# Three output panels worked abreast, k-tile by k-tile, at four stage changes of a two-block transformer kernel

## Chip, cores and metric

The kernel runs on one core of a Trainium2 chip. The metric is device time in microseconds (us) of one execution; lower is better. Below, PE is TensorE, DVE is VectorE, ACT is ScalarE, POOL is GpSimd and SP is SyncE.

## The reference

Two blocks follow each other on 256 tokens of width 1024, all in fp32. The first is an RMS norm, an input projection, several mixers (gated linear attention, cross attention) and an output projection. The second puts 16 meta tokens ahead (272 rows) and runs

```python
h = h + 0.5 * rmsnorm(swiglu(rmsnorm(h, n[0]), ffn1_wi[l], ffn1_wo[l]), n[1])
h = h + rmsnorm(hybrid_mixer(rmsnorm(h, n[2]), w_in[l], ...), n[3])
h = h + 0.5 * rmsnorm(swiglu(rmsnorm(h, n[4]), ffn2_wi[l], ffn2_wo[l]), n[5])
```

where swiglu multiplies by a 1024 x 5632 matrix and then by a 2816 x 1024 one, and hybrid_mixer begins with the projection of its normed input. What matters here is that each of these projections begins with a norm of the whole hidden state.

## The kernel before

Activations lie transposed, features on partitions: 8 k-tiles of 128 features by 256 or 272 columns (rows of the sequence). Weights come as panels of 1024 columns (one output tile of 128 features by 8 k-tiles). A panel passes a ring of 4 slots (RING): SP loads it into `raw`, ACT copies it to `whi` in a reduced-precision form (L648), POOL subtracts to get the rest, `wlo` (L553), and PE multiplies. The activation is split the same way, into `xh` (ACT) and `xl` (DVE). So each k-tile of an output costs three matmuls, and an output of 8 k-tiles costs 24, summed in one of four PSUM banks (`pb[o % 4]`).

`output` does one such output: it waits for the panel's `wlo` and for the bank (`open_output`), and then does the k-tiles in order. At a stage change its `each` argument makes each k-tile wait for its `xl`. DVE reads the finished bank, and only then is the bank free again.

The norm's scale is applied behind the matmuls, when a bank is read. Its statistic is the sum of squares: ACT squares each k-tile (`pre_norm`), POOL adds the squares (`sum_squares`), PE sums over partitions (`norm_stat`, L1470), ACT takes the root (`pre_root`, L669 and L671) into `xrstd`. DVE reads no bank of the new stage before that.

Every engine works through its own list in the order in which it is written. This order sets when panels are ready. On ACT the panels of a new stage are copied up to LEAD = 3 ahead, so its first three are split when the stage begins; the copy of the fourth stands behind `pre_root` in ACT's list:

```python
            pre_norm(3, combined(0), "gains", 0, WOUT_O + 7)
            pre_root(3)
            ...
            ahead(UP1_P - 1)
            up_loop(0, UP1_O, LEN)
```

`ahead(UP1_P - 1)` reaches panel UP1_P + 2, and the first `high_in_loop` of `up_loop` copies panel UP1_P + 3. A copy also waits until the panel that held its slot has been multiplied (`passed`).

The four places of the change are the starts of: UP1 (44 outputs of 272 columns, norm 3), the mixer (12 qkv outputs of 272 columns, norm 5), OUT2 (the mixer's output projection, 8 outputs of 256 columns, without a norm ahead, its `xl` made from `mg`), and UP2 (44 outputs of 256 columns, norm 7). In the mixer, the step `("logits",)` multiplies `h` by the small `wba` (L1695) into `ba`, transposes that (L1701), and DVE and ACT make `grate` from it (`g_ready`); the step `("cumulate",)` waits for that. On DVE each qkv output is scaled into `pre` (L1272) and then convolved in three instructions (`conv_tile`: L1227, L1231, L1236). Behind OUT2 and the down projections DVE runs `take_in`: for each output a copy out of PSUM (L1009), its square (L1011) and a sum (L1016).

Of the kernel before, what the change touches and what calls it, by code (L numbers as in the profile page):

```python
# [5 lines left out]
ROWS = 256  # L6
META = 16
LEN = META + ROWS
KT = 8
# [6 lines left out]
RING = 4  # L16
LEAD = 3
# [8 lines left out]
OUT2_P = MIX_P + 56 + 12  # L26
# [6 lines left out]
OUT2_O = MIX_O + 56 + 24  # L33
# [136 lines left out]
MIX_OUT = mixer_outputs()  # L170
# [49 lines left out]
def build(nc, a):  # L220
# [3 lines left out]
    with ctx:  # L224
# [22 lines left out]
        xh = at("xh", take(KT * LEN), [P, KT, LEN], f32r)  # L247
        xl = at("xl", take(KT * LEN), [P, KT, LEN], f32r)
# [51 lines left out]
        qkv = at("qkv", ar, [P, 12, LEN])  # L300
# [51 lines left out]
        pb = [ctx.enter_context(nc.psum_tensor(f"panel{i}", [P, 512], f32)) for i in range(4)]  # L352
# [12 lines left out]
        passed = sem("passed")  # L365
# [80 lines left out]
        mg_low = sem("mg_low")  # L446
# [1013 lines left out]
        def _(pe):  # L1460
            M = nc.tensor.matmul

            def norm_stat(n):

                bank, use = aux("stat", n)
                y = squares_of(n)
                late = n in (2, 4, 6, 8)
                aux_open(use)
                pe.wait_ge(summed, n + 1)
                ins = M(bank[:, 0:W[n]], ones[:], y[:, 0, 0:W[n]], start=True, stop=not late)  # L1470
                if late:
                    pe.wait_ge(last_squared, n // 2)
                    ins = M(bank[:, 0:W[n]], ones[:], y[:, KT - 1, 0:W[n]], start=False, stop=True)
                if n == 0:
                    for rt in range(2):
                        ins = M(bank[:, ROWS + rt:ROWS + rt + 1], y[:, 0, P * rt:P * rt + P], ones[:, 0:1], start=True, stop=True)
                ins.then_inc(aux_full, 1)

            def products(bank, slot, pairs, hi_, lo_, c0, w, first, last, each=None):
                for m, (t, kk) in enumerate(pairs):  # L1480
                    if each is not None:
                        each(kk)
                    for n, (wt, x) in enumerate(((whi, hi_), (whi, lo_), (wlo, hi_))):
                        ins = M(bank[:, 0:w], wt[:, slot, P * t:P * t + P], x[:, kk, c0:c0 + w],  # L1484
                                start=first and m == 0 and n == 0, stop=last and m == len(pairs) - 1 and n == 2)
                return ins

            def tiles_split(n):

                return lambda kk: pe.wait_ge(split_low, 8 * SPLIT[n] + kk + 1)  # L1490

            def open_output(o, p):

                pe.wait_ge(lo_ready, p + 1)
                if o >= 4:
                    pe.wait_ge(bank_free[o % 4], o // 4)

            def output(o, p, hi_, lo_, w, c0=0, tiles=KT, half=0, each=None):

                open_output(o, p)  # L1500
                pairs = [(tiles * half + t, t) for t in range(tiles)]
                products(pb[o % 4], p % RING, pairs, hi_, lo_, c0, w, True, True, each).then_inc(passed, 1)

            def output_rows(o, p, hi_, lo_):


                if p % 2:
                    return
                open_output(o, p)
                open_output(o + 1, p + 1)  # L1510
                r = p % RING
                for rt in range(2):
                    for kk in range(KT):
                        for n, (wt, x) in enumerate(((whi, hi_), (whi, lo_), (wlo, hi_))):
                            ins = M(pb[(o + rt) % 4][:, 0:2 * P], x[:, kk, P * rt:P * rt + P],  # L1515
                                    wt[:, r:r + 2, P * kk:P * kk + P], start=kk == 0 and n == 0, stop=kk == KT - 1 and n == 2)
                ins.then_inc(passed, 2)
# [29 lines left out]
            for step in FIRST:  # L1547
                kind, i = step[0], step[-1]
                if kind == "lowrank":
                    bank, n = aux("lowrank")  # L1550
                    aux_open(n)
                    for kk in range(KT):
                        ins = M(bank[0:16, 0:ROWS], wglr[:, kk, :], tmp[:, kk, 0:ROWS], start=kk == 0, stop=kk == KT - 1)
# [3 lines left out]
                if kind == "decay":  # L1557
                    aux_freed(pe, AUX[("lowrank",)])
                    for x in range(2):
                        bank, n = aux("up", x)  # L1560
                        aux_open(n)
                        for t in range(2):
                            ins = M(bank[:, 256 * t:256 * t + 256], upw[:, P * (2 * x + t):P * (2 * x + t) + P], glr[:],
                                    start=True, stop=True)
                        ins.then_inc(aux_full, 1)
                if kind == "level":
# [7 lines left out]
                    for x in range(2):  # L1574
                        if l == 8 and x:
                            break
                        bank, n = aux("level", l, g, x)
                        aux_open(n)
                        for m in range(4):
                            if l < 8:  # L1580
                                hd, blk = 4 * g + 2 * x + m // 2, slice(P * (m % 2), P * (m % 2) + P)
                                ins = M(bank[:, P * m:P * m + P], k[:, hd, blk], q[:, hd, blk], start=True, stop=True)  # L1582
                            else:
                                ins = M(bank[:, P * m:P * m + P], k[:, 4 * g + m, 0:P], q[:, 4 * g + m, P:ROWS], start=True, stop=True)
# [5 lines left out]
                if kind == "scores":  # L1590
                    st, pair = i // 2, i % 2
                    bank, n = aux("scores", i)
# [4 lines left out]
                    for e in range(2):  # L1597
                        ins = M(bank[:, ROWS * e:ROWS * e + ROWS], xq[:, 2 * pair + e, P * st:P * st + P], mk[:, 2 * pair + e, :],
                                start=True, stop=True)
                    ins.then_inc(aux_full, 1)  # L1600
                if kind == "probs":
                    bank, n = aux("probs", i)
# [4 lines left out]
                if kind == "o":  # L1607
                    bank, n = aux("o", i)
# [14 lines left out]
                    for e in range(2):  # L1623
                        if i < 6:
# [4 lines left out]
                            ins = M(bank[:, ROWS * e + P:ROWS * e + ROWS], v[:, 1, col:col + P], s[:, hd, P:ROWS],  # L1629
                                    start=False, stop=True)  # L1630
# [6 lines left out]
                if kind == "o_norm":  # L1637
                    bank, n = aux("o_norm", i)
# [13 lines left out]

            def up_loop(first_o, first_p, w, norm):

                output(first_o, first_p, xh, xl, w, each=tiles_split(norm))
                norm_stat(norm)
                for n in range(1, 4):
                    output(first_o + n, first_p + n, xh, xl, w)
                with pe.Fori(0, UP // 4 - 1) as g:
                    for n in range(4):  # L1660
                        pe.wait_ge(lo_ready, g * 4 + (first_p + 4 + n + 1))
                        pe.wait_ge(bank_free[n], g + (first_o // 4 + 1))
                        products(pb[n], n, [(t, t) for t in range(KT)], xh, xl, 0, w, True, True).then_inc(passed, 1)
# [21 lines left out]
            for step in MIXER:  # L1685
# [17 lines left out]
                if kind == "cumulate":  # L1703
# [3 lines left out]
                    for d in range(2):  # L1707
                        M(bank[0:CH, 16 * d:16 * d + 16], tri[:, d, :], grate[:, :, 4 * d:4 * d + 4], start=True, stop=True)
                    M(bank[0:CH, 32:64], ones[0:CH, 0:CH], small2[0:CH, 96:128], start=True, stop=True).then_inc(aux_full, 1)
                if kind in ("qkv", "fourier_in", "sconv"):  # L1710
                    output(o, p, xh, xl, LEN, each=tiles_split(5) if step == ("qkv", 0) else None)
                    if step == ("qkv", 0):
                        norm_stat(5)
                if kind in ("z", "gate"):
                    output(o, p, xh, xl, ROWS, META)
                if kind == "branch":
# [132 lines left out]
                if kind == "delta_norm":  # L1849
                    for e in range(2):  # L1850
# [3 lines left out]
                        for m in range(2):  # L1854
                            ins = M(bank[:, ROWS * m:ROWS * m + ROWS], ones[:], dsq[:, 2 * e + m, :], start=True, stop=True)
                        ins.then_inc(aux_full, 1)
            for i in range(8):
                output(OUT2_O + i, OUT2_P + i, xh, xl, ROWS, each=(lambda kk: pe.wait_ge(mg_low, kk + 1)) if i == 0 else None)
            norm_stat(6)
            up_loop(UP2_O, UP2_P, ROWS, 7)  # L1860
            down_loop(1, DOWN2_O, DOWN2_P, ROWS)
# [119 lines left out]
```

## Time and profile before

| | before |
|---|---|
| median of 3 executions | 1151.41 us (1149.96 to 1151.47) |
| span of the profiled execution | 1152.5 us |
| PE busy | 1028.8 us, 89% of the span |
| POOL busy | 746.5 us, 65% |
| DVE busy | 640.1 us, 56% |
| ACT busy | 472.7 us, 41% |

The profile is of one execution. Its span, from the first instruction to the last, is all the time that is known of it; it stands 1.1 us above the median. A matmul's row lasts longer than its share of PE, since matmuls overlap: the pace is the distance between the starts of neighbours. Two matmul rows stand for one fp32 product (L1470, L1695).

### The profile page before, as it was taken

Reading aid. Unit: us, or ns where it says so; the run is one execution under the profiler, and the core shown is the slowest. Engines: PE = TensorE matmul, PEld = TensorE weight load, DVE = VectorE, ACT = ScalarE, POOL = GpSimd, SP = SyncE. Lnnn points to the kernel's source line nnn. Section 1 sums busy time; section 2 is a strip of 40 time slices with the busy share of each in tenths; the row PEclk is TensorE's granted clock in tenths of the full one; section 3 lists DMA queues with packets and bytes.
Section 4 is the critical chain, followed back from the end, with each engine's and each line's share of the span. In section 5 each row is a group of like instructions: output and inputs, shape, how many; then the busy total and the mean of one; then the engine's idle time right before and its main releaser. Section 6 shows DMA issues by size and latency. Waiting matters only on the chain.

```text
span 1152.5 us, 21258 instructions
## 1 busy us (share of the span) xinstructions
PE 1028.8 (89%) x8096; PEld 998.8 (87%) x8096; DVE 640.1 (56%) x1026; ACT 472.7 (41%) x698; POOL 746.5 (65%) x349
## 2 busy tenths in 40 slices
PE   5799999989899999997988294999999869999996
PEld 4699999989799999996988174999999859999995
DVE  6324994447755554447955053345555585666454
ACT  5344224444454444444464012433325445444441
POOL 3786555647778878984767022655635757888993
PEclk9899999999899999997988696999998978999998
DMA  7454333425445555652441122443323633665561
GB/s 254 135 176 134 117 119 119 132 90 164 147 144 167 167 179 165 189 181 86 147 134 51 5 60 48 146 133 107 97 87 94 199 110 116 197 183 183 173 196 66
DMA packets 52368, 155.44 MB, mean 135 GB/s; under 512 B 10228, under 2 KB 15612, under 8 KB 52108
## 3 DMA queue, kind: packets, MB, share of 16 engines
q1 hardware_dynamic: 45504, 151.28, 42.3%
q10 hardware_dynamic: 6800, 3.25, 1.2%
q8 instruction: 47, 0.77, 0.3%
q14 instruction: 17, 0.14, 0.0%
HBM read 152.11 MB, written 2.39 MB: 134 GB/s over the span
## 4 chain that ended last, share of the span: by engine, by line
PE 75%; DVE 15%; ACT 3%; ACTq 3%; DMA 1%; issue 1%; POOL 1%; DVEq 0%; SPq 0%
PE panel L1484 58%; PE panel L1515 4%; PE aux L1582 2%; ACTq L871 2%; DVE xl L968 1%; PE aux L1771 1%; DVE qkv L1231 1%; DVE qkv L1236 1%; ACTq L885 1%; DVE qkv L1227 1%; DVE pr L1313 1%; DMA tm<-inverses 1%; DVE h L983 1%; POOL wlo L553 1%; DVE tmp L978 1%
## 5 line engine op out<-in xcount | busy, mean ns | idle before, releaser
L553 POOL TENSOR_TENSOR wlo<-raw,whi 128x1024 fp32r<-128x1024 f32 x284 | 700.5, 2486 | 343.1 <-ACT whi L648 343.1
L1484 PE MATMUL panel<-xh,whi 128*128 128x256 f32 (+1 forms) x1504 | 443.6, 295 | 27.0 <-DVE xl L968 18.8
L1484 PE MATMUL panel<-xl,whi 128*128 128x256 f32 (+1 forms) x1504 | 435.3, 289 | 0.0
L1484 PE MATMUL panel<-xh,wlo 128*128 128x256 f32 (+1 forms) x1504 | 434.3, 289 | 0.0
L648 ACT ACTIVATE whi<-raw 128x1024 fp32r<-128x1024 f32 x284 | 294.0, 1052 | 204.8 <-PE panel L1484 148.8
L1484 PEld LDWEIGHTS panel<-xh,whi 128*128 128x128 f32 x1504 | 291.7, 194 | 35.8 <-DVE xl L968 14.2
L1484 PEld LDWEIGHTS panel<-xh,wlo 128*128 128x128 f32 x1504 | 291.7, 194 | 0.0
L1484 PEld LDWEIGHTS panel<-xl,whi 128*128 128x128 f32 x1504 | 291.2, 194 | 0.5
L1484 PE MATMUL panel<-hh,whi 128*128 128x272 f32 (+1 forms) x352 | 100.1, 284 | 0.0
L1484 PE MATMUL panel<-hh,wlo 128*128 128x272 f32 (+1 forms) x352 | 99.9, 284 | 0.0
L1484 PE MATMUL panel<-hl,whi 128*128 128x272 f32 (+1 forms) x352 | 99.8, 284 | 0.0
L1206 DVE TENSOR_TENSOR hl<-hid,hh 128x272 f32 (+1 forms) x44 | 53.4, 1213 | 32.9 <-ACT hh L795 32.9
L1204 DVE TENSOR_TENSOR hid<-hid,sil 128x272 f32<-128x272 f32 (+1 forms) x44 | 66.1, 1502 | 6.6 <-ACT sil L793 1.0
L795 ACT ACTIVATE hh<-hid 128x272 f32 (+1 forms) x44 | 18.7, 425 | 123.2 <-DVE hid L1204 123.2
L1484 PEld LDWEIGHTS panel<-hl,whi 128*128 128x128 f32 x352 | 66.4, 189 | 0.0
L1484 PEld LDWEIGHTS panel<-hh,wlo 128*128 128x128 f32 x352 | 66.2, 188 | 0.0
L1484 PEld LDWEIGHTS panel<-hh,whi 128*128 128x128 f32 x352 | 66.1, 188 | 0.0
L1200 DVE TENSOR_TENSOR hid<-panel,xrstd 128x272 f32<-128x272 f32 (+1 forms) x44 | 19.1, 433 | 65.1 <-PE panel L1484 65.1
L1009 DVE COPY tmp<-panel 128x256 f32<-128x256 f32 (+1 forms) x24 | 10.3, 430 | 76.0 <-PE panel L1484 75.9
L1016 DVE TENSOR_TENSOR sq<-sq 128x256 f32<-128x256 f32 (+1 forms) x24 | 44.4, 1850 | 0.8
L1484 PE MATMUL panel<-mixh,whi 128*128 128x256 f32 x128 | 37.3, 292 | 4.1 <-DVE mixl L1178 4.1
L1771 PE MATMUL aux<-cmat,pf 68*128 68x256 f32 x64 | 18.2, 448 | 22.2 <-DVE pf L1339 22.2
(286 smaller groups left out, 1603.2 us busy)
## 6 DMA issues: line engine op xcount, KB each, us to landing
raw<-in_panels SPq DMA_DIRECT2D x236, 512.0 KB, 3.5
raw<-in_down SPq DMA_DIRECT2D x32, 448.0 KB, 3.3
raw<-in_down SPq DMA_DIRECT2D x16, 512.0 KB, 3.6
memx<-in_mem SPq DMA_DIRECT2D x1, 1024.0 KB, 5.1
h<-in_x SPq DMA_DIRECT2D x1, 1024.0 KB, 8.2
spill<-h ACTq DMA_DIRECT2D x1, 1024.0 KB, 6.2
h<-spill ACTq DMA_DIRECT2D x1, 1024.0 KB, 7.3
out<-h SPq DMA_DIRECT2D x2, 512.0 KB, 2.9
```

Of the source, the lines that this page charges most:

```text
L553: nc.gpsimd.tensor_tensor(wlo[:, slot, :], raw[:, slot, :], whi[:, slot, :].bitcast(f32), ALU.subtract).then_inc(lo_ready, 1)
L648: A(whi[:, slot, :], raw[:, slot, :], ACT.Copy).then_inc(hi_ready, 1)
L795: A(hh[:, bass.ds(tile, 1), 0:w].rearrange("p a s -> p (a s)"), hid[:, pair, 0:w], ACT.Copy).then_inc(hid_high, 1)
L871: act.dma_start(a["blocks"][b].rearrange("m i j -> i m j"), am[at_b, :, :, at_b].rearrange("i u h j -> i (u h) j")).then_inc(blocks_in, 16)
L1016: ins = TT(sq[:, 0, 0:W[n]], sq[:, 0, 0:W[n]], sq[:, i, 0:W[n]], ALU.add)
L1200: TT(hid[:, pair, 0:w], pb[2 * pair + 1][:, 0:w], xrstd[:, 0:w], ALU.mult)\
L1204: TT(hid[:, pair, 0:w], hid[:, pair, 0:w], sil[:, pair, 0:w], ALU.mult).then_inc(hid_ready, 1)
L1206: TT(hl[:, bass.ds(tile, 1), 0:w].rearrange("p a s -> p (a s)"), hid[:, pair, 0:w], hh[:, bass.ds(tile, 1), 0:w].rearrange("p a s -> p (a ...
L1484: ins = M(bank[:, 0:w], wt[:, slot, P * t:P * t + P], x[:, kk, c0:c0 + w], start=first and m == 0 and n == 0, stop=last and m == len(pairs ...
L1515: ins = M(pb[(o + rt) % 4][:, 0:2 * P], x[:, kk, P * rt:P * rt + P], wt[:, r:r + 2, P * kk:P * kk + P], start=kk == 0 and n == 0, stop=kk ...
L1582: ins = M(bank[:, P * m:P * m + P], k[:, hd, blk], q[:, hd, blk], start=True, stop=True)
L1771: ins = M(bank[:, 0:ROWS], pf[:, i % 2, c, P * cs:P * cs + P], cmat[:, c, cs, :], start=x == 0 and m == 0, stop=x == 1 and m == 3)
```

## The change

A new function `outputs_abreast` opens three outputs (three banks, three panels), and then does, for each k-tile, three matmuls for each of them. It takes the place of `output` for the first three outputs at the four places. `norm_stat` now stands behind all three. In the mixer, qkv 1 and qkv 2 are done with qkv 0, ahead of the logits, and the steps `("qkv", 1)` and `("qkv", 2)` leave PE nothing to do.

```diff
+            def outputs_abreast(outputs, hi_, lo_, w, each):
+
+                for o, p in outputs:
+                    open_output(o, p)
+                for kk in range(KT):
+                    each(kk)
+                    for o, p in outputs:
+                        ins = products(pb[o % 4], p % RING, [(kk, kk)], hi_, lo_, 0, w, kk == 0, kk == KT - 1)
+                        if kk == KT - 1:
+                            ins.then_inc(passed, 1)
...
             def up_loop(first_o, first_p, w, norm):
 
-                output(first_o, first_p, xh, xl, w, each=tiles_split(norm))
+                outputs_abreast([(first_o + n, first_p + n) for n in range(LEAD)], xh, xl, w, tiles_split(norm))
                 norm_stat(norm)
-                for n in range(1, 4):
+                for n in range(LEAD, 4):
                     output(first_o + n, first_p + n, xh, xl, w)
...
-                if kind in ("qkv", "fourier_in", "sconv"):
-                    output(o, p, xh, xl, LEN, each=tiles_split(5) if step == ("qkv", 0) else None)
-                    if step == ("qkv", 0):
-                        norm_stat(5)
+                if step == ("qkv", 0):
+                    outputs_abreast([MIX_OUT[("qkv", n)][:2] for n in range(LEAD)], xh, xl, LEN, tiles_split(5))
+                    norm_stat(5)
+                elif kind in ("qkv", "fourier_in", "sconv") and step not in (("qkv", 1), ("qkv", 2)):
+                    output(o, p, xh, xl, LEN)
...
-            for i in range(8):
-                output(OUT2_O + i, OUT2_P + i, xh, xl, ROWS, each=(lambda kk: pe.wait_ge(mg_low, kk + 1)) if i == 0 else None)
+            outputs_abreast([(OUT2_O + i, OUT2_P + i) for i in range(LEAD)], xh, xl, ROWS, lambda kk: pe.wait_ge(mg_low, kk + 1))
+            for i in range(LEAD, 8):
+                output(OUT2_O + i, OUT2_P + i, xh, xl, ROWS)
```

The order of instructions changes on PE alone; DVE, ACT and SP have the same lists before and after, and POOL's differs in nothing but line numbers. On PE at UP1, before, the last k-tile of the first output, the statistic (L1470), and then the second output (panel1 is its bank):

```order
L1484 MATMUL panel0<-xh_52,whi_50 128x272 [waits split_low]
L1484 MATMUL panel0<-xl_53,whi_50 128x272
L1484 MATMUL panel0<-xh_52,wlo_51 128x272
L1470 MATMUL aux0<-sq_56,ones_61 128x272 [waits summed,aux_free0]
L1484 MATMUL panel1<-xh_52,whi_50 128x272 [waits bank_free1,lo_ready]
L1484 MATMUL panel1<-xl_53,whi_50 128x272
L1484 MATMUL panel1<-xh_52,wlo_51 128x272
```

Of the change, the last k-tile of all three, the statistic, and then the fourth output:

```order
L1484 MATMUL panel0<-xh_52,whi_50 128x272 [waits split_low]
L1484 MATMUL panel0<-xl_53,whi_50 128x272
L1484 MATMUL panel0<-xh_52,wlo_51 128x272
L1484 MATMUL panel1<-xh_52,whi_50 128x272
L1484 MATMUL panel1<-xl_53,whi_50 128x272
L1484 MATMUL panel1<-xh_52,wlo_51 128x272
L1484 MATMUL panel2<-xh_52,whi_50 128x272
L1484 MATMUL panel2<-xl_53,whi_50 128x272
L1484 MATMUL panel2<-xh_52,wlo_51 128x272
L1470 MATMUL aux0<-sq_56,ones_61 128x272 [waits summed,aux_free0]
L1484 MATMUL panel3<-xh_52,whi_50 128x272 [waits bank_free3,lo_ready]
```

The statistic has moved behind six more matmuls of the last k-tile (and behind 48 more in all), and what follows it is the output of the fourth panel, which waits for that panel's `wlo`.

On PE at the mixer's start, before, the end of qkv 1, the logits (L1695, then the transposes of `ba`, L1701), and qkv 2 (panel2):

```order
L1484 MATMUL panel1<-xh_52,whi_50 128x272
L1484 MATMUL panel1<-xl_53,whi_50 128x272
L1484 MATMUL panel1<-xh_52,wlo_51 128x272
L1695 MATMUL aux3<-h_54,wba_64 16x272 [waits wba_scaled,aux_free3]
L1695 MATMUL aux3<-h_54,wba_64 16x272 x7
L1701 MATMUL aux0<-ident_60,ba_119 68x16 [waits aux_free0,aux_free3]
L1701 MATMUL aux0<-ident_60,ba_119 68x16 x3
L1484 MATMUL panel2<-xh_52,whi_50 128x272 [waits bank_free2,lo_ready]
```

Of the change, the end of the three, the statistic, the logits (now L1706 and L1712), the cumulate step (L1719, which waits for `g_ready`), and qkv 3 (panel3):

```order
L1484 MATMUL panel2<-xh_52,whi_50 128x272
L1484 MATMUL panel2<-xl_53,whi_50 128x272
L1484 MATMUL panel2<-xh_52,wlo_51 128x272
L1470 MATMUL aux2<-sq_56,ones_61 128x272 [waits summed,aux_free2]
L1706 MATMUL aux3<-h_54,wba_64 16x272 [waits wba_scaled,aux_free3]
L1706 MATMUL aux3<-h_54,wba_64 16x272 x7
L1712 MATMUL aux0<-ident_60,ba_119 68x16 [waits aux_free0,aux_free3]
L1712 MATMUL aux0<-ident_60,ba_119 68x16 x3
L1719 MATMUL aux1<-small2_117,tri_65 68x16 [waits g_ready,aux_free1]
L1719 MATMUL aux1<-small2_117,tri_65 68x16
L1720 MATMUL aux1<-small2_117,ones_61 68x32
L1484 MATMUL panel3<-xh_52,whi_50 128x272 [waits bank_free3,lo_ready]
```

Nothing stands any longer between the statistic and the logits, nor between the logits and the cumulate step, where qkv 1 and qkv 2 stood.

## Rows read from the trace of the kernel before

**Rows 1.** Page, the chain that ended last, shares by engine.

```profile
PE 75%; DVE 15%; ACT 3%; ACTq 3%; DMA 1%; issue 1%; POOL 1%; DVEq 0%; SPq 0%
```

**Rows 2.** Waits, whole trace, then 903 to 960: who waited for whom, us, times, longest.

```profile
PE panel L1484 <- DVE xl L968: 18.8, 20, 3.8
...
PE panel L1484 <- DVE xl L1450: 4.2, 2, 2.5
```

**Rows 3.** Chain in order of time: start us, us, what; changes to UP1 and UP2.

```profile
316.57 1.73 PE panel L1484 x6
...
319.20 196.28 PE panel L1484 x1560
...
952.52 1.65 PE panel L1484 x6
...
955.02 185.65 PE panel L1484 x1560
```

**Rows 4.** Timeline at UP1: start us, us, engine, line, op, [idle before <-releaser].

```profile
308.74 0.36 PE L1484 MATMUL panel<-xh,whi 128*128 128x272 f32 x1 [2.80 <-DVE xl L968]
...
315.51 1.41 DVE L968 SCALAR_TENSOR_TENSOR xl<-h,vec,xh 128x272 fp32r<-128x272 f32 x2
...
319.24 0.49 ACT L669 ACTIVATE lnt<-aux,vec 128x272 f32<-128x272 f32 x1 [2.77 <-PE aux L1470]
...
321.50 2.01 ACT L648 ACTIVATE whi<-raw 128x1024 fp32r<-128x1024 f32 x2
...
322.65 20.13 POOL L553 TENSOR_TENSOR wlo<-raw,whi 128x1024 fp32r<-128x1024 f32 x8 [5.10 <-ACT whi L648]
```

**Rows 5.** Windows: us, PE busy, PEclk, DMA share, GB/s; the granted clock.

```profile
319.00:320.00 1.00, 1.00 (x8) 0.81 0.00 0
...
520.00:521.00 1.00, 0.00 (x0) 0.88 0.00 0
...
916.00:917.00 1.00, 1.00 (x7) 0.65 0.00 0
...
957.00:958.00 1.00, 1.00 (x8) 0.67 0.00 0
```

**Rows 6.** Timeline at UP1, PE: two neighbouring matmuls at the lower clock.

```profile
317.41 0.43 PE L1484 MATMUL panel<-xh,whi 128*128 128x272 f32 x1
...
317.64 0.43 PE L1484 MATMUL panel<-xl,whi 128*128 128x272 f32 x1
```

**Rows 7.** Timeline at the mixer's start.

```profile
536.88 3.84 PE L1695 MATMUL aux<-h,wba 128*16 128x272 f32 x16
...
534.53 0.44 DVE L1272 TENSOR_TENSOR pre<-panel,xrstd 128x272 f32<-128x272 f32 x1 [3.37 <-ACT xrstd L671]
...
537.47 0.93 DVE L1227 TENSOR_SCALAR qkv<-pre,vec 128x272 f32<-128x272 f32 x1
...
538.32 2.58 DVE L1231 SCALAR_TENSOR_TENSOR qkv<-pre,vec,qkv 128x271 f32<-128x271 f32 x1
...
540.82 0.42 DVE L1247 TENSOR_TENSOR ba<-aux,xrstd 16x272 f32<-16x272 f32 x1
...
535.87 4.73 POOL L553 TENSOR_TENSOR wlo<-raw,whi 128x1024 fp32r<-128x1024 f32 x2 [4.07 <-ACT whi L648]
```

**Rows 8.** Timeline: POOL, four splits back to back, and one VectorE operation among them.

```profile
550.07 10.02 POOL L553 TENSOR_TENSOR wlo<-raw,whi 128x1024 fp32r<-128x1024 f32 x4 [0.68 <-ACT whi L648]
...
552.78 2.64 DVE L1236 SCALAR_TENSOR_TENSOR qkv<-pre,vec,qkv 128x271 f32<-128x271 f32 x1
```

**Rows 9.** Timeline at OUT2.

```profile
908.33 0.36 PE L1484 MATMUL panel<-xh,whi 128*128 128x256 f32 x1 [2.47 <-DVE xl L1450]
...
912.42 0.39 PE L1484 MATMUL panel<-xh,whi 128*128 128x256 f32 x1 [1.73 <-DVE xl L1450]
...
913.50 1.06 ACT L648 ACTIVATE whi<-raw 128x1024 fp32r<-128x1024 f32 x1 [4.01 <-PE panel L1484]
...
914.63 2.37 POOL L553 TENSOR_TENSOR wlo<-raw,whi 128x1024 fp32r<-128x1024 f32 x1 [2.55 <-ACT whi L648]
...
933.20 2.37 POOL L553 TENSOR_TENSOR wlo<-raw,whi 128x1024 fp32r<-128x1024 f32 x1 [0.27 <-ACT whi L648]
...
937.61 0.42 DVE L1011 TENSOR_TENSOR sq<-tmp 128x256 f32<-128x256 f32 x1
```

**Rows 10.** Timeline at UP2, POOL.

```profile
958.43 14.94 POOL L553 TENSOR_TENSOR wlo<-raw,whi 128x1024 fp32r<-128x1024 f32 x6 [4.98 <-ACT whi L648]
```

## The prediction

> **What bounds the kernel now.** I read the page's chain first. PE holds 75% of it [rows 1], so time is won where PE waits with work at hand. The list of waits says how much of that lies at the stage changes: PE waited 18.8 us in all for an `xl` of a norm, and 4.2 us for an `xl` of OUT2 [rows 2]. That is what the change can fill. The chain in order of time then shows what follows such a wait: from 319.20 on, 1560 matmuls in 196.28 us without a break, 0.126 us each, and at UP2 1560 from 955.02 in 185.65 us, 0.119 each [rows 3]. So in UP1 and UP2 every microsecond by which PE starts its unbroken run earlier is won, and every one later is lost. Then the timelines of the other engines at the four places, to see what that run waits for.
>
> **The term that decides: the fourth panel.** The change brings forward two outputs, 48 matmuls or 6.0 us at UP1. But PE can go on only if the fourth panel is split by then. In ACT's list its copy stands behind the root of the statistic: Ln at 319.24, table load, copies from 321.50, and POOL takes the first at 322.65, after 5.10 us without work [rows 4]. At 20.13/8 = 2.5 us a split, it is ready at 325.15. Before, PE had outputs 2 and 3 to do in that time: 319.20 + 48 x 0.126 = 325.25 [rows 3]. The cover fits to a tenth. Now both are done ahead of the statistic, and the cover is gone: PE stands still from the statistic to the fourth panel, 5.9 us (325.15 - 319.24). What is saved ahead of the statistic is given back behind it, but for the shift of the statistic itself.
>
> **The clock.** Where PE has idled, its granted clock falls: at 520 to 521 PE is idle and the mean clock 0.88, so it fell in that microsecond from 2.4 GHz to 1.2 (0.5) [rows 5]. It rises again under work. At UP1 unbroken work began at 316.57 [rows 3] and the clock rose at 319.4 (0.81 in that microsecond is 38% at 0.5), 2.8 us later; at OUT2, where a pause of 1.73 us brought the lower clock, at 912.42 [rows 9] and 916.7, 4.3 us; at UP2 at 952.52 and 957.7, 5.1 us [rows 3, 5]. I take 4.0 us, bounds 2.8 and 5.1. A matmul of 272 columns takes 0.225 us at the lower clock (317.41 to 317.64, rounded) [rows 6] against 0.126, so 4.0 us there cost 4.0 x (1 - 0.126/0.225) = 1.8 us (1.2 to 2.2). After 5.9 us of idleness the fourth output starts at the lower clock, and nothing hides that: it heads the unbroken run.
>
> **UP1: +2.6.** The first matmul is at 308.74 [rows 4]. 72 matmuls: 4.0 us at 0.225 do 17.8, the other 54.2 take 6.8 us, more than the k-tiles need to arrive (the last `xl` ends at 316.92) [rows 4]. They end at 319.55. The statistic's two matmuls take 0.5 (3.84/16 each at the full clock) [rows 7], so it ends at 320.05 against 319.20: 0.85 late. ACT, and POOL behind it, shift by as much, and the fourth output starts at 326.1 where it started at 325.25. With the clock: 0.85 + 1.8 = +2.6 us. Bounds with 2.8 and 5.1: +1.5 and +3.6.
>
> **UP2: +1.0.** Here k-tiles come slower, and the last two set the end: 18 matmuls from 952.52 take 2.1 us at the full clock, the statistic 0.5: 955.15 against 955.02. The fourth panel is ready at 958.43 + 2.5 + 0.15 = 961.1 [rows 10]. Before, the fourth output started at 955.02 + 2.64 at 0.213 (12.4 matmuls; 0.225 x 256/272) + 35.6 x 0.119 = 961.9. So PE begins 0.8 earlier, and pays 1.8 for the clock: +1.0 (+0.4 to +1.6).
>
> **OUT2: +1.4.** No norm stands here, and PE does gain: the three outputs run without a break from 908.33, the wait of 1.73 at 912.42 [rows 9] is filled, and no idleness lowers the clock. They end at 908.33 + 72 x 0.119 = 916.9. But the first output now ends at 908.33 + 66 x 0.119 + 0.3 = 916.5, not 913.4, and the copy of the fifth panel waits for exactly that (ACT, 913.50, released by PE). POOL's row of splits, which began at 914.63, begins at 917.6; the copies of two more panels are released at once, and from then POOL runs seven splits back to back. They set what DVE can do: a VectorE operation with its inputs in SBUF that meets a split waits for its end. In the mixer four splits took 10.02 us, 2.5 each, and the operation among them 2.64 instead of 0.42 to 0.49 [rows 8]; 538.32 shows the same [rows 7]. Seven splits end at 935.1 (before 935.57). `take_in` has 14 such operations. The first fits in ahead of the splits, seven pass, one a split, and six are left behind them, with three copies: nine at 0.455 us are 4.1 us, so it ends at 939.4 (935.1 + 0.3 + 4.1, rounded down), against 938.03 [rows 9]. PE's last output would be done by 916.9 + 5 x 2.85 = 931.2. If operations slip between splits, it is less. If VectorE were not held at all, `take_in` would follow PE; before, the three outputs ended at about 912.42 + 54 x 0.119 + 1.8 (the clock) = 920.6, so PE is some 3.5 us earlier. I take +1.4, ends -3.5 and +2.0, near the held end because the rows are of two-input operations like these.
>
> The Trainium skill (SBUF — State Buffer, Who interferes with whom) has the rule for it: a VectorE instruction with two SBUF inputs contends with a GpSimd one that reads SBUF. The trace agrees (2.64 us). The same section says that the order of issue decides who is blocked; if VectorE came first each time, OUT2 would be worth its -3.5 and the whole sum 0.1 us. In rows 7 and 8 it was VectorE that was held.
>
> **The mixer's start: 0.** DVE sets the pace here. The statistic is 0.3 late by the reckoning of UP2. qkv 1 is then at hand, so its operations move up from 537.47 to about 536.1, just where POOL's first split starts (535.87 + 0.3). If the scaling (L1227) slips in first, the next operation is held by one split and not by the second, and `ba` comes at 538.8 and not 540.82, -2.0. If it doesn't, `ba` comes at 541.3, +0.5 [rows 7]. The logits' matmuls (3.84 us) used to follow qkv 1, and now follow the statistic and end at 537.8, in time. But PE has then only small work until `g_ready`, and qkv 3 runs at the lower clock: 24 matmuls take 4.8 us, not 3.0, and DVE may wait up to 1 us for it. Range -2.0 to +1.5; between two cases of unlike sign I take 0.
>
> **Parts at no cost.** Opening three outputs at once needs three panels split: OUT2's third is the closest, and PE begins only after DVE's first `xl`, when it is. Their banks have long been read. PE changes banks between k-tiles elsewhere at the same pace. SP and the DMAs follow `wlo`; a load has at least one split of 2.5 us to spare.
>
> **Sum.** 2.6 + 0 + 1.4 + 1.0 = +5.0 us. The profiled span of 1152.5 us becomes 1157.5. It stands 1.1 above the median, so the median of 1151.4 becomes 1156.4. A measurement tells about 0.2%, 2.3 us, from no change.
>
> **Rivals.**
> 1. *VectorE keeps up at OUT2, and the mixer falls well.* -3.5 to 0 at OUT2 and -2 to 0 in the mixer, beside +3.6 of UP1 and UP2: from -1.9 up to the edge of what can be told, +2.3, so 1149.5 to 1153.7. In its middle, 1151.6, it is no change. For: some operations before a split began passed at 0.42. Chance 0.20.
> 2. *The change pays (other side).* It needs one thing: that the clock survives the 5.9 us of idleness at UP1 and UP2, or that the matmuls abreast reach the full clock sooner than the sparse ones did. Then UP1 is +0.85 or less, UP2 -0.8, and with PE's gain at OUT2, -3.5, the sum is -3.5, 1148; it decides from a clock that costs under 1 us a place. Against: rows 5 show it fall while PE idled, and the pause of 1.73 us at OUT2 was enough. Chance 0.10.
> 3. *The clock stays low through the whole of the matmuls abreast*, because PE still pauses for k-tiles. 72 x 0.225 = 16.2 us: UP1's statistic ends near 308.74 + 16.2 + 1 = 326, 6.8 late; the mixer's and UP2's, with slower k-tiles, some 5 late each. With OUT2 and the clock behind the idleness the sum is about +20, 1171. Against: with nine matmuls a k-tile at 0.225, 2.0 us, and a k-tile every 1.3 to 1.7, PE has no pauses while it is slow, and unbroken work raised the clock in all three rows. Chance 0.05. The Trainium skill speaks for this rival (TensorE: Matmul & The Clock Gate, "A second HAM failure mode: psum-queue depth-cycling"): a kernel that cycled through PSUM banks paused PE often enough between groups that its clock went up and down. No run here shows it for groups that stand back to back.
> 4. *The change doesn't do what it says*, PE still waits as before: excluded by the order, which has nine matmuls between waits.
>
> **Chances.** Forecast 0.65 (1153.7 to 1160), rivals 0.20, 0.10, 0.05. Faster by over 0.2%: rival 2 and the low end of rival 1, 0.10. Within: 0.22. Slower: 0.68. The range for 8 in 10 runs from 1152 (leaves rival 2 and half of rival 1) to 1160 (the bounds of the terms, 3.6 + 1.6 + 2.0 + 1.5 = 8.7).
>
> **What the new profile would show.** PE idle 5 to 6 us behind L1470 at UP1 and UP2, released by POOL `wlo`, and the clock at 0.5 behind it; the waits for `xl` at a third or less. At OUT2, POOL without a gap and L1011 and L1016 at 2.5 us each. Wrong would be: no idle PE behind the statistic (the fourth panel came another way), or a clock of 1.0 there.

## The result, and the profile after

The changed kernel takes 1157.68 us in the median (1157.21 to 1158.83, 4 runs), beside 1151.44 us for the kernel before on the same chip (1149.96 to 1153.64, 4 runs). The ratio is 1.0055, 95% interval 1.0038 to 1.0071: slower by 6.2 us by the medians. I had put 1156.4, range 1152 to 1160.

The page, the chain by engine, and the list of waits (who waited for whom, us in total, times, longest), changed kernel:

```profile
PE 75%; DVE 12%; ACT 4%; ACTq 3%; issue 2%; POOL 2%; DMA 1%; DVEq 0%; SPq 0%; POOLq 0%
...
PE panel L1484 <- POOL wlo L553: 27.1, 6, 13.1
...
PE panel L1484 <- DVE xl L968: 11.4, 7, 3.8
```

DVE's share of the chain fell from 15% to 12% [rows 1] and PE's wait for `xl` from 18.8 us to 11.4 [rows 2]: the change did what it was made for. What came in its place is in the same two rows. POOL's share went from 1% to 2%, "issue" from 1% to 2%, and PE waits 27.1 us for `wlo` where it waited 18.3 before; some 14 us of either sum belong to the start of the program, and the two new waits are of 5.8 us each.

The waits for `xl` did not fall to "a third or less". At each of the four places PE waits once for the first k-tile, 2.5 to 3.8 us, and bringing other outputs forward cannot fill that; of the 20 waits of norms before, 7 are left, and these carry 11.4 of the 18.8 us.

The chain in order of time (start us, us, what), changed kernel, at UP1 and UP2:

```profile
316.42 6.65 issue
...
323.11 2.35 POOL wlo L553
...
325.51 192.03 PE panel L1484 x1512
...
953.76 6.02 issue
...
959.81 2.35 POOL wlo L553
...
962.21 181.35 PE panel L1484 x1512
```

Before, the unbroken run was 1560 matmuls from 319.20 [rows 3]. Now it is 1512, two outputs fewer, and begins at 325.51, behind POOL's split. The timeline of ACT and POOL there (start us, us, engine, line, op, [idle before <-releaser]):

```profile
319.71 0.49 ACT L669 ACTIVATE lnt<-aux,vec 128x272 f32<-128x272 f32 x1 [3.54 <-PE aux L1470]
...
321.97 2.00 ACT L648 ACTIVATE whi<-raw 128x1024 fp32r<-128x1024 f32 x2
...
323.11 7.42 POOL L553 TENSOR_TENSOR wlo<-raw,whi 128x1024 fp32r<-128x1024 f32 x3 [5.84 <-ACT whi L648]
```

The whole row of ACT and POOL has moved by about half a microsecond against [rows 4] (Ln from 319.24 to 319.71), and PE stands still from the statistic to the end of the first split: 325.46 - 319.71 = 5.8 us, where I had written 5.9. The clock in that stretch (window us, PE busy, PEclk, DMA share, GB/s):

```profile
320.00:321.00 1.00, 0.00 (x0) 1.00 0.00 0
...
322.00:323.00 1.00, 0.00 (x0) 0.73 0.00 0
...
329.00:330.00 1.00, 1.00 (x9) 0.85 0.69 94
```

It falls to 1.2 GHz while PE idles, and is back at 2.4 in the microsecond 329 to 330, some 4 us into the new run.

OUT2 of the changed kernel, timeline:

```profile
916.07 2.96 ACT L648 ACTIVATE whi<-raw 128x1024 fp32r<-128x1024 f32 x3 [7.00 <-PE panel L1484]
...
917.20 17.59 POOL L553 TENSOR_TENSOR wlo<-raw,whi 128x1024 fp32r<-128x1024 f32 x7 [4.84 <-ACT whi L648]
...
917.26 2.63 DVE L1011 TENSOR_TENSOR sq<-tmp 128x256 f32<-128x256 f32 x1
...
919.93 2.51 DVE L1016 TENSOR_TENSOR sq<-sq 128x256 f32<-128x256 f32 x1
...
922.47 0.43 DVE L1009 COPY tmp<-panel 128x256 f32<-128x256 f32 x1
...
938.66 0.43 DVE L1011 TENSOR_TENSOR sq<-tmp 128x256 f32<-128x256 f32 x1
```

POOL's first split went from 914.63 [rows 9] to 917.20, seven stand back to back, and every square and sum that meets one takes 2.0 to 2.6 us. The copy between them, which reads PSUM, takes 0.43. The mixer's start, changed kernel:

```profile
538.31 4.97 POOL L553 TENSOR_TENSOR wlo<-raw,whi 128x1024 fp32r<-128x1024 f32 x2 [4.40 <-ACT whi L648]
...
538.49 2.59 DVE L1231 SCALAR_TENSOR_TENSOR qkv<-pre,vec,qkv 128x271 f32<-128x271 f32 x1
...
541.00 0.42 DVE L1247 TENSOR_TENSOR ba<-aux,xrstd 16x272 f32<-16x272 f32 x1
...
551.29 0.44 DVE L1272 TENSOR_TENSOR pre<-panel,xrstd 128x272 f32<-128x272 f32 x1 [1.86 <-PE panel L1484]
```

Only one operation is held, by the first of the two splits. Before, it was held by the second, and the scaling ahead of it by half a microsecond by the first [rows 7].

Where the time went shows best in the length of stages. Each number is the distance between two rows: the starts of ACT's exponentials (L671) that bound a stage, of ACT's first square of qkv in the mixer (L841), and of PE's first matmul of OUT2. "Before again" is the kernel before, profiled once more beside the experiments.

| stage, us | before | before again | after |
|---|---|---|---|
| norm 2 to UP1's root | 13.27 | 13.26 | 14.06 |
| UP1's root to norm 4 | 198.26 | 198.94 | 199.84 |
| norm 4 to the mixer's root | 15.98 | 15.98 | 16.38 |
| mixer's root to its first L841 | 29.55 | 29.87 | 26.82 |
| OUT2: first matmul to norm 6 | 31.64 | 28.74 | 33.11 |
| norm 6 to UP2's root | 15.60 | 15.59 | 15.93 |
| UP2's root to norm 8 | 187.31 | 187.06 | 188.81 |

### The profile page after: what moved, and what is told of

Read it like the earlier page. It is cut to its first block, busy times and chain, and to the rows that moved or that the text cites. A ratio compares the mean times of both kernels' runs of the same rounds, so it can differ in the third digit from the quotient of the medians.

```text
span 1155.4 us, 21258 instructions
## 1 busy us (share of the span) xinstructions
PE 1021.2 (88%) x8096; PEld 995.0 (86%) x8096; DVE 640.0 (55%) x1026; ACT 472.4 (41%) x698; POOL 746.4 (65%) x349
## 4 chain that ended last, share of the span: by engine, by line
PE 75%; DVE 12%; ACT 4%; ACTq 3%; issue 2%; POOL 2%; DMA 1%; DVEq 0%; SPq 0%; POOLq 0%
PE panel L1484 59%; PE panel L1526 4%; PE aux L1593 2%; ACTq L871 2%; POOL wlo L553 1%; PE aux L1783 1%; DVE xl L968 1%; ACTq L885 1%; DVE sq L1011 1%; DVE pr L1313 1%; DMA tm<-inverses 1%; DVE tmp L978 1%; DVE h L983 1%; DVE sq L1016 1%; PE aux L1840 1%
## 5 line engine op out<-in xcount | busy, mean ns | idle before, releaser
L1206 DVE TENSOR_TENSOR hl<-hid,hh 128x272 f32 (+1 forms) x44 | 50.5, 1148 | 32.9 <-ACT hh L795 32.9
L1016 DVE TENSOR_TENSOR sq<-sq 128x256 f32<-128x256 f32 (+1 forms) x24 | 48.5, 2021 | 0.8
```

Of the source, the lines that this page charges most:

```text
L1016: ins = TT(sq[:, 0, 0:W[n]], sq[:, 0, 0:W[n]], sq[:, i, 0:W[n]], ALU.add)
L1206: TT(hl[:, bass.ds(tile, 1), 0:w].rearrange("p a s -> p (a s)"), hid[:, pair, 0:w], hh[:, bass.ds(tile, 1), 0:w].rearrange("p a s -> p (a ...
```

## Experiments

Each was timed against the kernel before on the same chip. The stage lengths are those of the one profiled execution of each kernel.

### The kernel before, once more

> The kernel before, unchanged, measured against itself on the same chip: 0 us within 0.2%. It shows how far two profiles of one kernel differ stage by stage, which the comparison of the single profiles of before and after needs; I expect the mixer to differ by up to 3 us and the other stages by under 0.5.

1151.47 us (12 runs), ratio 1.0003, 0.999 to 1.0016. But its single executions lie between 1148.9 and 1156.0, and the profiled one has a span of 1148.5, 4.0 less than the profile that I had argued from. Two stages are shorter by more than that: 2.7 us in the mixer between the l2 norm and `zs` (62.97 and 65.68), where nothing was changed, and 2.9 at OUT2; the others add 1.6 the other way. OUT2 in this execution:

```profile
906.90 2.76 DVE L1450 TENSOR_TENSOR xl<-mg,xh 128x256 fp32r<-128x256 f32 x8
...
933.83 0.43 DVE L1011 TENSOR_TENSOR sq<-tmp 128x256 f32<-128x256 f32 x1
```

The eight `xl` take 2.76 us in one go. In my profile a split fell among them, they took 4.93, PE paused for 1.73 us and its clock fell to the lower level (0.50 at 914 to 915) [rows 9]. Of the profiles with OUT2 in the old order and nothing changed there, this one and that of the mixer's start alone have 28.7 us; mine has 31.64, and two more, each the slowest execution of its kernel, 30.1 and 30.6. I had taken a slow draw for the stage's length. The split among the `xl` is not the whole of it: in the 30.1 the eight `xl` took 2.76 us too, and what made that stage longer stays open.

### UP1 and UP2 alone

Only `up_loop` has the three abreast:

```diff
-                output(first_o, first_p, xh, xl, w, each=tiles_split(norm))
+                outputs_abreast([(first_o + n, first_p + n) for n in range(LEAD)], xh, xl, w, tiles_split(norm))
                 norm_stat(norm)
-                for n in range(1, 4):
+                for n in range(LEAD, 4):
```

> Only the starts of UP1 and UP2 work three outputs abreast; the mixer and OUT2 are as before. Theory (the fourth panel's split stands behind the statistic, PE idles some 6 us and then starts at the lower clock): +3.6 us against before, between +2 and +6, with PE idle over 5 us in front of POOL's wlo at both places. Rival (the change pays where a norm's k-tiles are waited for, and the loss is at OUT2 or the mixer): -2 us or less.

1154.16 us (10 runs), ratio 1.0026, 1.0015 to 1.0038: +3.0. As forecast in kind and nearly in size (+3.6). The profiled execution is the slowest of the ten (1162.06), but its two stages behind the root, 200.19 and 189.20 us, are within 0.4 of those of the changed kernel, so they can be compared.

### The mixer's start alone

The same edit only at `("qkv", 0)`.

> Only the mixer's start is abreast. Prediction: 0 us, between -2.0 and +1.5. The two profiles of before and after say -2.5 us for this stage, if they can be compared. Rival: the statistic's lateness and qkv 3 at the lower clock pass straight on to VectorE's convolution, +1 to +2 us.

1149.94 us (12 runs), ratio 0.9984, 0.9971 to 0.9997: -1.8. The order pays here. The first of the two cases that I had weighed is what happens, in this run's profile as in the changed kernel's: both scalings slip in ahead of the split, and one operation (L1231, 2.59 us) is held instead of two.

### OUT2 alone

> Only OUT2 is abreast. Theory (seven splits back to back hold take_in's VectorE operations): +1.4 us, between 0 and +2, with L1011 and L1016 at 2.5 us while POOL splits, and POOL without a gap. Rival (PE bounds the stage): -3.3 us.

1155.72 us (6 runs), ratio 1.0034, 1.0022 to 1.0046: +3.9, the largest single loss, where I had +1.4. The stage is 33.10 us, as in the changed kernel; against my profile's 31.64 that is +1.5, against 28.74 it is +4.4. The measured +3.9 puts the usual length before at 29.2, near the short form.

### The fourth panel's copy moved ahead

This tests what the wait at UP is made of. In ACT's and POOL's lists the fourth panel's copy and split go ahead of the stage change (a loop over 24 down panels is written out so that the panels behind keep their order):

```diff
 # GpSimd
-            ahead(WOUT_P + 15)
+            ahead(UP1_P)
             sum_squares(3)
-            loop(UP + 24)
+            loop(UP + 20)
+            ahead(MIX_P - 1)
...
-            ahead(OUT2_P + 7)
+            ahead(UP2_P)
             sum_squares(7)
 # ScalarE
+            ahead(UP1_P)
             post_root(2)
...
+            ahead(UP2_P)
             nc.scalar.preload_act_table_set(LN_EXP)
             post_root(6)
```

With UP1 and UP2 abreast:

> The three outputs abreast at UP1 and UP2 alone, and there the fourth panel's copy and its split moved ahead of the stage change: ScalarE copies it as soon as the last output before the stage has passed, GpSimd splits it before it adds the squares. The run with the two UP stages abreast and nothing else measured 1154.2 us against 1151.5 for the kernel before (+3.0 from its ratio). Theory (what is lost at UP is not the order of the products but the fourth panel, which can only be copied behind the statistic): after the statistic PE has one whole output, 24 matmuls or 2.9 us, to work on while the fifth panel is copied and split, so each place gives back 2.9, and the clock's 1.8 as well if the wait that is left (about 2.4 us) is too short to lower it: 1148.4 without the clock's part, 1144.8 with it, range 1144.5 to 1150. Rival (the late statistic and the reading of the banks that hangs on it set the time): 1153 to 1154.5, the copies change nothing. Second rival: the early split falls beside VectorE's take-in and holds it, +1 to +2 at each place, 1150 to 1153.

1151.57 us beside 1152.46 for the kernel before, ratio 0.9999, 0.9988 to 1.0009. Of the +3.0 all is gone, so the fourth panel was the term. But in the whole time 3 us came back, where I had expected 5.8 without the clock's part and 9.4 with it. One reason is in the new clock windows at UP1, another at OUT2, in the next experiment.

```profile
323.00:324.00 1.00, 0.96 (x8) 1.00 0.00 0
324.00:325.00 1.00, 0.00 (x0) 1.00 0.00 0
...
326.00:327.00 1.00, 0.14 (x1) 0.85 0.00 0
327.00:328.00 1.00, 1.00 (x5) 0.50 0.65 49
...
330.00:331.00 1.00, 1.00 (x9) 0.95 0.78 82
```

PE works up to 324, stands for the fifth panel until 326.9, and the shorter wait still ends in the lower clock. The stage from UP1's root to norm 4 is 196.71 us (200.19 in the run without the copies), UP2's 185.18 (189.20): 3.5 and 4.0 us less, where the panel alone was to give 2.9 each. 0.5 was given back ahead of the statistic: the early split (305.82 to 308.16) holds VectorE's first L1181, which takes 1.07 us where it took 0.50.

In the kernel before, with nothing abreast:

> The same early copy and split of the fourth panel at UP1 and UP2, in the kernel before (nothing abreast). There PE does not wait for a panel after the stage's first output, so nothing is gained: 1151.5, range 1150.5 to 1152.5. If the split is in VectorE's way at the stage change: +0.5 to +2, 1152 to 1153.5. If the copies themselves had been a hidden limit: below 1150.

1154.88 us, ratio 1.0021, 1.0012 to 1.003: +2.4, more than I gave the copies alone. The early copy is of no use there, and it costs. At OUT2 the added split, the last of the row, meets a sum that would have been free (timeline):

```profile
933.85 2.34 POOL L553 TENSOR_TENSOR wlo<-raw,whi 128x1024 fp32r<-128x1024 f32 x1 [0.30 <-ACT whi L649]
...
933.87 2.60 DVE L1013 TENSOR_TENSOR sq<-sq 128x256 f32<-128x256 f32 x1
```

The stage takes 30.92 us, +2.2 against 28.74. In the mixer the stages differ by about 1 us in either direction, which this experiment does not explain. The kernel with the copies and the UP stages abreast has the same 30.92 us at OUT2, so its 0.9999 holds this loss of 2.2 too, and the copies give the UP stages more than the 3.0 that it shows. Between the two kernels with the copies, the one with the UP stages abreast is the faster by 2.5 us (0.9999 against 1.0021): with the panel at hand, the order itself pays.

### PE kept busy in the wait

This tests the clock alone. Behind the statistic, with UP1 and UP2 abreast and the copies as they were:

```diff
                 norm_stat(norm)
+                pe.wait_ge(bank_free[(first_o + LEAD) % 4], (first_o + LEAD) // 4)
+                for _ in range(40):
+                    M(pb[(first_o + LEAD) % 4][:, 0:w], xl[:, 0, 0:P], xh[:, 0, 0:w], start=True, stop=True)
```

> The two UP stages abreast, and behind the statistic 40 matmuls more into the fourth bank, whose results the fourth output overwrites: they take about 4.6 us at the higher clock out of the 5.8 us in which PE waits for the fourth panel, and change nothing else. Theory (of the 3.0 that the UP stages cost, 1.8 at each place is the clock that falls in this wait): the granted clock stays high into the loop, 1154.2 less 3.6 is 1150.6, range 1150 to 1152. Rival (the clock is lowered by the wait before the statistic, or doesn't matter because the loop is bound by something else): 1153.5 to 1154.5. If the 40 matmuls run at the lower clock they take 9 us and end behind the fourth panel: up to 3 more at each place, 1157 to 1160.

```profile
326.00:327.00 1.00, 0.73 (x6) 1.00 0.00 0
327.00:328.00 1.00, 0.40 (x3) 1.00 0.00 0
328.00:329.00 1.00, 1.00 (x10) 1.00 0.47 57
```

The clock stays at 2.4 GHz at both places, and the stages behind the root take 198.23 and 186.49 us, 2.0 and 2.7 less than the 200.19 and 189.20 of the same kernel without the 40 matmuls. Against the changed kernel's 199.84 and 188.81 it is 1.6 and 2.3. That is the clock's price, and I had put 1.8 at each. The whole time says less. 1154.29 us, ratio 1.0011, 1.0 to 1.0022, lies in the rival's range and not in mine; it is 1.7 less than without the 40 matmuls by the ratios, and the two intervals together leave anything from nothing to 3.5. So the price of the clock rests on the records of one execution of each kernel. That of this kernel was the slowest of twelve; part of its excess stands in the chunked recurrence (234.2 us from the first L1313 to OUT2, 228.1 to 230.5 in the others), far from the edit. Ahead of UP1's root its stage is 0.8 longer than the changed kernel's (14.90 and 14.06): there the clock was low from 308.1 to 314.9, ahead of and among the matmuls abreast, and in the changed kernel only from 308.8 to 312.2.

### OUT2 abreast, with the squares read from PSUM

This tests the hold. VectorE's square takes one input from PSUM instead of both from SBUF:

```diff
-                        CP(y, pb[o % 4][:, 0:W[n]]).then_inc(bank_free[o % 4], 1)
-                    ins = TT(sq[:, i, 0:W[n]], y, y, ALU.mult)
+                        order(CP(y, pb[o % 4][:, 0:W[n]]))
+                        ins = TT(sq[:, i, 0:W[n]], pb[o % 4][:, 0:W[n]], y, ALU.mult)
+                        ins.then_inc(bank_free[o % 4], 1)
```

> OUT2 alone abreast, as in the run that measured 1155.7 (+3.9), and VectorE's squares there and at the two other take-ins of copied outputs (after DOWN1 and DOWN2) computed from PSUM and SBUF instead of twice from SBUF, for seven of the eight outputs; the bank is freed by the square. Theory (at OUT2 abreast GpSimd's splits come without a gap, and an operation of VectorE with both inputs in SBUF is held until a split ends, while one that reads PSUM is not): L1011 falls from 2.0 to 2.6 us to about 0.45, each of four outputs costs VectorE about 3.0 instead of 5.1, and the stage is then bound by the splits: 4 less, 1151.5, range 1150 to 1153. Rival (both operations are held whatever they read, or PE waits for the splits and not for the banks): 1155 to 1156.

1151.22 us, ratio 0.9997, 0.9982 to 1.0011; OUT2 falls from 33.10 to 28.46 us, -4.6. The timeline:

```profile
915.99 17.60 POOL L553 TENSOR_TENSOR wlo<-raw,whi 128x1024 fp32r<-128x1024 f32 x7 [4.84 <-ACT whi L648]
...
919.18 0.42 DVE L1012 TENSOR_TENSOR sq<-panel,tmp 128x256 f32<-128x256 f32 x1
919.64 1.59 DVE L1022 TENSOR_TENSOR sq<-sq 128x256 f32<-128x256 f32 x1
```

POOL's row is the same to 0.01 us. The square, now with one input in SBUF, passes in 0.42; the sum behind it, with both, is still held, to the end of the same split. The loss at OUT2 is this hold. It is the rule that the Trainium skill gives (SBUF — State Buffer, Who interferes with whom): a VectorE instruction with two SBUF inputs contends with a GpSimd one that reads SBUF, one with at most one such input does not, outside VectorE's 2-port modes. The trace agrees (1.59 and 2.63 us with two, 0.42 with one).

And in the kernel before, in the old order:

> The kernel before, nothing abreast, with VectorE's squares of the three take-ins read from PSUM and SBUF. Theory (the holds of OUT2 cost the kernel before little, since its splits leave gaps of 0.3 to 0.45 us and PE is only late by them at the end, but in some executions the stage takes 31.6 instead of 28.7): 0 to 1 less, 1150.5 to 1151.5 for a before of 1151.5. Rival (the squares are the limit of the whole stage in every execution): 2 or more less. If reading PSUM were the slower way: above 1152.

1149.09 us beside 1151.85, ratio 0.9975, 0.9959 to 0.9992: -2.9, not the 0 to 1 that I expected; the rival, that the squares limit the stage in every execution, was right. OUT2 takes 25.39 us, 3.3 less than 28.74.

```profile
913.44 0.42 DVE L1022 TENSOR_TENSOR sq<-sq 128x256 f32<-128x256 f32 x1
...
913.65 2.47 POOL L553 TENSOR_TENSOR wlo<-raw,whi 128x1024 fp32r<-128x1024 f32 x1 [0.33 <-ACT whi L648]
```

In the old order each split waits for its output, as `take_in` does. With a square of 0.42 us, the sum starts 0.2 us ahead of the split and passes; with the held square it came too late and met it. So the order at OUT2 is worth 3.1 us (28.46 against 25.39), in favour of the old one, even when the squares are free. (The edit is also in the take-ins behind the two down projections, whose part in the 2.9 was not measured apart.)

### The change with its repairs

Copies and squares as above, and 16 matmuls behind the fourth output, in PE's wait for the fifth panel. First only UP1 and UP2 abreast, with copies and fill:

> UP1 and UP2 alone abreast, with the early copies and the 16 matmuls behind the fourth output. With the copies alone this measured a ratio of 0.9999; the records there show the clock at its lower level for about 4.2 us at UP1 and 3.2 us at UP2, beginning at the end of the 2.9 us in which PE waits for the fifth panel. Theory (that wait is what lowers it): the clock stays high at both places and 2 to 3 in all are given back: 1148.5 to 1149.5 for a before of 1151.5, ratio 0.998. Rival (the clock is of no account, the loop takes up the difference): 0.9995 to 1.0005.

1147.18 us beside 1151.85, ratio 0.9956, 0.9937 to 0.9975, lower than I had put it. The clock stays high (325 to 328 all at 1.00), and the two stages behind the root are 1.4 us shorter each than with the copies alone (195.33 and 183.73 us). By the ratios the fill is worth 4.9, by the records 2.8; the two intervals together leave 4.9 uncertain by 2.5, so the two do not contradict each other, and I hold with the records.

Then all four places, and all four but OUT2:

> The change as it was made, at all four places, with three repairs: at UP1 and UP2 the fourth panel's early copy and split; behind the fourth output 16 matmuls more into a bank that the fifth overwrites, about 1.9 us of the wait for the fifth panel; and VectorE's squares read from PSUM and SBUF. Taken against a before of 1151.5. Theory (the change loses by the fourth panel's copy, by the clock in the wait for it and by VectorE's holds at OUT2, each of which a repair takes away, and gains at the mixer's start): the early copies alone brought the UP stages from +3.0 to 0, the fill gives 1 to 2 more at each, the mixer's start 1.8, and OUT2 stands at 0: 1151.5 less 3 less 1.8 is 1146.7, range 1145 to 1149. Rival (the repairs get in each other's way: the eighth split at OUT2 and the early copies hold VectorE there): 1149 to 1152. Were the losses elsewhere than I put them: 1154 and above.

> The same as the repaired kernel, but OUT2's outputs one after the other as before. Theory (with the squares from PSUM OUT2 abreast measured 0 against before, so the order there is worth nothing either way): 1146.7, within 1 of the repaired kernel on the same chip. Rival (splits back to back at OUT2 still cost, or still save by the xl subtractions being worked under): over 1.5 apart, lower if the order still costs.

1143.40 and 1142.81 us beside 1151.85, ratios 0.9918 (0.9897 to 0.9939) and 0.9918 (0.9895 to 0.994). Both are below the 1146.7 forecast, and below its range. For the first the records give 2.2 us of the 3.3: the "0" that I took for the UP stages with the copies held the loss at OUT2 (30.92 against 28.74), and here OUT2 takes 28.46. The two differ by 0.6 us in the median, which says nothing; in the records OUT2 is 2.5 us longer abreast (28.46 and 25.93), the other changed stages are equal to 0.2. So the change, slower by 6.2 us as made, is part of a kernel that is faster by 8.5. Not all of that is the order's: the squares from PSUM gave the kernel before 2.9 by themselves, and the early copies, without the order, cost it 2.4. With copies and fill but without the squares, UP1 and UP2 abreast gave 4.7 (1147.18 against 1151.85).

## Why the prediction held, and where it did not

**The fourth panel.** Right, and it is what decides. The wait is 5.8 us for 5.9; with the panel copied early the loss of 3.0 is gone.

**The clock behind it.** Right: it fell while PE idled, and holding PE busy kept it up. At UP2 it was under-priced (2.3 to 2.7 against 1.8): it stayed low from the start of the new run at 962.2 to 967.6, 5.4 us, where I had taken 4.0.

**UP1 +2.6 and UP2 +1.0.** Together 3.6, measured 3.0 (1.7 to 4.4 from the interval). In the records UP1 is +2.4 against my profile and +1.7 against the one taken again, UP2 +1.8 and +2.1. The statistic was late by 0.79 us for 0.85 at UP1, by 0.33 for 0.13 at UP2.

**OUT2 +1.4.** The mechanism is right, the size is not. "Seven splits end at 935.1" (917.20 + 17.59 = 934.8), "it ends at 939.4" (939.09). The step that failed is the other side of the difference: "against 938.03". That end was of one execution, with a pause among the `xl` that the short form of the stage (28.74 us) does not have; against 31.64 the 33.11 us abreast are +1.5, as forecast. Against the median it is +3.9.

**The mixer's start 0.** Of two cases of unlike sign I took the middle. The first came, in every profile with this order: -1.8 measured. Its two halves are as written: `ba` 4.0 us behind the scaled bank and not 6.3, and PE late for the fourth output (1.86 us at 551.29, for "up to 1"), with the clock at 0.50 from 545 to 551.

**The parts at no cost.** "PE changes banks between k-tiles elsewhere" was no reading: in the kernel before these products change banks only between panels. In the changed kernel it changes after every three matmuls, and from 313 to 319 they follow each other at 0.125 us, where I had used 0.126, so nothing is indeed the right size for it.

**The sum.** +5.0 forecast. The parts measured give 3.0 - 1.8 + 3.9 = +5.1, the whole 6.2, interval 4.4 to 8.2. The sum was right partly by luck: two errors, +2.5 at OUT2 and -1.8 in the mixer, nearly cancel. The base had an error too: the time of an execution is its span and 1.8 us more (1155.4 and 1157.21 for the changed kernel, 1148.5 and 1150.33 for the kernel before again), so the profiled execution of before stood some 2.9 us above the median, not 1.1. That does not move the forecast, 1151.4 and 5.0; the same slow execution is what gave OUT2 its wrong length. A profile that far off its median should have warned me that some stage of it was not typical.

**The signs.** The idle PE behind the statistic, the clock behind it and POOL without a gap came as written; the waits for `xl` did not (11.4 of 18.8 us).

**The rivals.** The first (VectorE keeps up at OUT2) is out: it was held seven times. Its other half, that the mixer falls well, is what happened. The second (the clock survives) is out by the windows. The third (clock low through the matmuls abreast) too: at 318 to 319 it is at 1.00.

## What to carry to other kernels

Work that is brought forward across a wait is no longer there to cover what comes behind the wait. Before pulling it, find what it was hiding (here a weight panel whose copy stands in another engine's list behind the same event), and move that first. Where one engine's operations hold another's, as splits hold `take_in` here, the phase between them is part of the schedule: a change that lets one run without gaps can cost more on the other than it gives (+3.9 us at OUT2). And take stage lengths from more than one execution before a difference of 1 to 3 us is built on them.

## What I had not expected of the hardware

The hold depends on where the operands lie, to the instruction: 1.6 to 2.6 us for squares and sums with both inputs in SBUF that meet a split, 0.42 for copies and products that read PSUM, among the same splits. But one input in SBUF is not always safe. The scaling L1227 (one input and one output, both fp32 in SBUF) took 0.36 us free, 2.19 beside a split at 545.34 in the kernel before, and 4.03 at 546.97 in the run with the copies alone (L1224 there), to the end of a split and of the memset behind it (550.83). And a start 0.2 us ahead of a split was enough to pass.

The spread of single executions of one kernel (1147.7 to 1154.8 for before in 28 runs) is wide, and in the two profiles of it the largest differences are lumps of 2.7 and 2.9 us at single stages, not noise over all of them; two profiles cannot show that it is always so.
